# Second attention of a two-block transformer kernel: scores as two stacked products over both halves of the partitions, copies by transfers, row maxima added as a row

## The reference

```
q, k = rms_norm(q per head) * q_gain, rms_norm(k per head) * k_gain
c = cumsum(log_sigmoid(f_logit + b_f))           # one running sum per head
s = (q @ k.T) * 64**-0.5 + (c_q[:, None] - c_k[None, :])
s = where(pos_k <= pos_q, s, -inf)
p = softmax(s, axis=-1)
o = (p @ v) * sigmoid(gate);  out = o @ w_out
```

## Time and profile before

| | |
|---|---|
| runs before, median (lowest to highest) | 1735.58 us (1731.82 to 1736.38) |
| the profiled execution's own time | 1730.72 us |
| its span, first to last instruction | 1728.8 us |
| PE busy, share of the span | 1661.1 us, 96% |
| PEld / DVE / ACT / POOL busy | 79% / 53% / 36% / 6% |
| mean granted TensorE clock | 0.983 of full |
| chain of waits that ended last | PE 84%, DVE 10%, ACT 3%, issue 1%, DMA 1% |
| attention's heads in the span | about 1181 to 1316 us |

### The profile page before, as it was taken

One profiled execution on the slowest core, in us unless ns is written; L12 is line 12 of the kernel. 1 busy time (PEld: TensorE's weight loads), 2 busy tenths in 40 slices (PEclk: granted clock), 3 DMA queues, 4 the chain that ended last, 5 costly groups with the idle time before them and its releaser, 6 DMA issues.

```text
span 1728.8 us, 20336 instructions
## 1 busy us (share of the span) xinstructions
PE 1661.1 (96%) x8091; PEld 1357.3 (79%) x8091; DVE 913.3 (53%) x1256; ACT 615.5 (36%) x789; POOL 96.1 (6%) x134
## 2 busy tenths in 40 slices
PE   8899979899999899999999999999999999999997
PEld 3478858778887688888888889977877878888885
DVE  5755585577666644444344564145656544444333
ACT  2332357522223333333333443235553422222221
POOL 0100000111110000000000100003430000000000
PEclk9989989999999899999999999999999999999998
DMA  9322100555644133332333321231112333332331
GB/s 323 117 89 71 49 25 25 179 172 163 204 161 146 49 99 97 97 97 83 101 94 113 104 74 51 74 103 53 39 31 63 84 98 98 98 97 67 101 101 49
DMA packets 213924, 170.28 MB, mean 98 GB/s; under 512 B 5444, under 2 KB 202948, under 8 KB 213830
## 3 DMA queue, kind: packets, MB, share of 16 engines
q1 hardware_dynamic: 207222, 144.80, 28.2%
q0 software_dynamic: 6608, 24.19, 4.2%
HBM read 166.84 MB, written 2.13 MB: 98 GB/s over the span
## 4 chain that ended last, share of the span: by engine, by line
PE 84%; DVE 10%; ACT 3%; issue 1%; DMA 1%; DVEq 0%; SPq 0%; POOLq 0%; POOL 0%; ACTq 0%
PE PS L436 23%; PE PS L437 23%; PE PS L438 23%; PE PS L2173 2%; DVE WL L92 2%; DVE T L92 1%; PE PS L563 1%; ACT WH L88 1%; PE PS L2156 1%; PE PS L2148 1%; PE PS L2149 1%; PE PS L2150 1%; PE PS L2129 1%; PE PS L457 0%; PE PS L1188 0%
## 5 line engine op out<-in xcount | busy, mean ns | idle before, releaser
L436 PE MATMUL PS<-XH,WH 128*128 128x512 f32 (+1 forms) x1280 | 488.8, 382 | 9.3 <-DVE WL L92 8.3
L437 PE MATMUL PS<-XL,WH 128*128 128x512 f32 (+1 forms) x1280 | 485.1, 379 | 0.0
L438 PE MATMUL PS<-XH,WL 128*128 128x512 f32 (+1 forms) x1280 | 484.9, 379 | 0.0
L92 DVE TENSOR_TENSOR WL<-WS,WH 128x2048 fp32r<-128x2048 f32 (+1 forms) x129 | 272.4, 2112 | 222.8 <-ACT WH L88 220.6
L436 PEld LDWEIGHTS PS<-XH,WH 128*128 128x128 f32 x1280 | 240.6, 188 | 57.7 <-DVE WL L92 11.8
L438 PEld LDWEIGHTS PS<-XH,WL 128*128 128x128 f32 x1280 | 240.0, 188 | 45.6
L437 PEld LDWEIGHTS PS<-XL,WH 128*128 128x128 f32 x1280 | 240.5, 188 | 43.7
L88 ACT ACTIVATE WH<-WS 128x2048 fp32r<-128x2048 f32 (+1 forms) x129 | 228.6, 1772 | 74.9 <-PE PS L438 51.2
L436 PE MATMUL PS<-HH,WH 128*128 128x512 f32 x352 | 137.0, 389 | 0.2 <-DVE WL L92 0.2
L437 PE MATMUL PS<-HL,WH 128*128 128x512 f32 x352 | 136.9, 389 | 0.0
L438 PE MATMUL PS<-HH,WL 128*128 128x512 f32 x352 | 136.9, 389 | 0.0
(11 more groups left out here) (361 smaller groups left out, 2363.0 us busy)
## 6 DMA issues: line engine op xcount, KB each, us to landing
WS<-in_w_in SPq DMA_DIRECT2D x24, 1024.0 KB, 5.4
WS<-in_ffn_w_up SPq DMA_DIRECT2D x44, 512.0 KB, 5.1
WS<-in_ffn_w_in SPq DMA_DIRECT2D x44, 512.0 KB, 5.0
MSRC<-in_w_mod POOLq DMA_DIRECT2D x32, 512.0 KB, 4.8
WS<-in_fox_w_in SPq DMA_DIRECT2D x16, 1024.0 KB, 5.6
WS<-in_ffn_w_down SPq DMA_DIRECT2D x16, 704.0 KB, 4.7
WS<-in_ffn_w_out SPq DMA_DIRECT2D x16, 704.0 KB, 4.7
MODW<-in_w_mod SPq DMA_DIRECT2D x8, 1024.0 KB, 10.9
```

Source lines behind the costliest of these rows:

```text
L92: self.e.tensor_tensor(o, a, b, op).then_inc(*self.done.to(*key))
L436: e.matmul(o, lh, rh, start=first and i == 0, stop=False)
L437: e.matmul(o, lh, rl, start=False, stop=False)
L438: ins = e.matmul(o, ll, rh, start=False, stop=last and i == n - 1)
```

## The change

The scores of a tile become three products. Two tiles of both halves are stacked: `KLH[., x]` holds the low keys in the head's own half and the high keys in the other half, `QHL[., x]` the high queries in its own half and the low queries in the other, so that one product over 128 partitions gives both cross terms. `KHZ` x `QHZ` is the high product, and in the half that was zero `KHZ` has a row of ones and `QHZ` the row of bounds, so that it subtracts the bound too. `SHIFT`, `ONER`, `QS` and `KLZ` go. What lies in the wrong half is brought there by SP: six transfers for each pair (`fx_pair_load`), and four for each head (`fx_shift_load`), each of which writes 128 bounds, one from each partition, into 512 bytes of one row. VectorE copies the bounds once for them (`BTR`). The rows' products read the own half of `QHZ` and `KHZ` alone: 64 partitions. ScalarE copies the high queries in two instructions for each pair, GpSimd makes the low ones in two. SP issues decay loads, pair loads and bound loads in a new order, and chunk `OUT2 + 2` after them, as `QHZ[0]` and `QHL[0]` lie in its landing slot.

```diff
@@ fx_split_act / fx_split_dve / fx_split_pool
-        a.act(QS[m % 2][:, :], QT[:, m, :], ACT.Copy, key=("fx_q_hi", m))
+        for x in range(2):
+            a.act(QHZ[m % 2][own(x), x, :], QT[own(x), m, :], ACT.Copy, key=("fx_q_hi", m, x))
...
-        g.e.wait_ge(*acts.at("fx_q_hi", m))
-        g.tt(QO[:, m, :], QT[:, m, :], QS[m % 2][:, :].bitcast(F32), ALU.subtract, key=("fx_q_lo", m))
+        for x in range(2):
+            g.e.wait_ge(*acts.at("fx_q_hi", m, x))
+            g.tt(QO[own(x), m, :], QT[own(x), m, :], QHZ[m % 2][own(x), x, :].bitcast(F32), ALU.subtract,
+                 key=("fx_q_lo", m, x))
@@ new
+    def fx_pair_load(e, m):
+        i, done = m % 2, landing(f"fx_pair{m % 2}")
+        for x in range(2):
+            e.wait_ge(*acts.at("fx_k_hi", m, x))
+            e.dma_start(KLH[i][own(1 - x), x, :].bitcast(F32), KHZ[i][own(x), x, :].bitcast(F32)).then_inc(done, 16)
+        for x in range(2):
+            e.wait_ge(*acts.at("fx_q_hi", m, x))
+            e.dma_start(QHL[i][own(x), x, :].bitcast(F32), QHZ[i][own(x), x, :].bitcast(F32)).then_inc(done, 16)
+        for x in range(2):
+            e.wait_ge(*pool.at("fx_q_lo", m, x))
+            e.dma_start(QHL[i][own(1 - x), x, :].bitcast(F32), QO[own(x), m, :].bitcast(F32)).then_inc(done, 16)
+    def fx_shift_load(e, h):
+        m, x = divmod(h, 2)
+        r = 64 - 64 * x
+        e.wait_ge(*dve.at("fx_shift", h))
+        for i in range(4):
+            row = QHZ[m % 2][r:r + 1, x, 128 * i:128 * i + 128].bitcast(F32)
+            e.dma_start(row, BTR[:, h % 4, i:i + 1].bitcast(F32)).then_inc(landing(f"fx_shift{h % 4}"), 16)
@@ fx_rows_pe
-            q = QS[m % 2][:, 128 * i:128 * i + 128]
+            q = QHZ[m % 2][own(x), x, 128 * i:128 * i + 128]
+            k = KHZ[m % 2][own(x), x, :]
@@ fx_scores_pe
-            e.wait_ge(*pool.at("fx_q_lo", m))
+            e.wait_ge(*landed(f"fx_pair{b}", 6 * (m // 2 + 1)))
...
-            e.matmul(o, kh[:, x, k0:k1], qh[:, q0:L], start=True, stop=False)
-            e.matmul(o, kh[:, x, k0:k1], ql[:, q0:L], start=False, stop=False)
-            e.matmul(o, kl[:, x, k0:k1], qh[:, q0:L], start=False, stop=False)
+            e.matmul(o, KLH[b][:, x, k0:k1], QHL[b][:, x, q0:L], start=True, stop=False)
             e.matmul(PS[0:KEYS[t], STOFF[t]:STOFF[t] + w], IDR[:, 0:KEYS[t]], AFTER[:, c:c + w], start=False, stop=False)
             if t == 0:
-                e.wait_ge(*pool.at("fx_shift", h))
-            ins = e.matmul(o, ONER[:, 0:KEYS[t]], SHIFT[h % 2][:, q0:L], start=False, stop=True)
+                e.wait_ge(*landed(f"fx_shift{h % 4}", 4 * (h // 4 + 1)))
+            ins = e.matmul(o, KHZ[b][:, x, k0:k1], QHZ[b][:, x, q0:L], start=False, stop=True)
@@ fx_max_dve
+        if h >= 4:
+            e.wait_ge(*landed(f"fx_shift{h % 4}", 4 * (h // 4)))
+        v.cp(BTR[:, h % 4, :], BT[:, h % 2, :], key=("fx_shift", h))
@@ sync
-        for j in range(PROJ + 3, OUT2 + 3):
+        for j in range(PROJ + 3, OUT2 + 2):
...
-        for h in range(16):
+        fx_decay_load(e, 0)
+        fx_pair_load(e, 0)
+        fx_shift_load(e, 0)
+        for h in range(1, 4):
             fx_decay_load(e, h)
-        for j in range(OUT2 + 3, NCH):
+        fx_pair_load(e, 1)
+        fx_shift_load(e, 1)
+        for h in range(14):
+            if h + 4 < 16:
+                fx_decay_load(e, h + 4)
+            fx_shift_load(e, h + 2)
+            if h % 2 and (h + 3) // 2 < 8:
+                fx_pair_load(e, (h + 3) // 2)
+        for j in range(OUT2 + 2, NCH):
             load_chunk(e, j)
```

More of the change, by code:

```diff
@@ L259, in build @@
     KHZ = [zone(f"KHZ{i}", [128, 2, NT], F32R, 52.5 + 4.125 * i) for i in range(2)]
-    KLZ = [zone(f"KLZ{i}", [128, 2, NT], F32R, 60.75 + 4.125 * i) for i in range(2)]
-    IDR, ONER, AFTER = (zone(n, [128, 128], F32R, 86.5 + 0.5 * i) for i, n in enumerate(("IDR", "ONER", "AFTER")))
+    KLH = [zone(f"KLH{i}", [128, 2, NT], F32R, 60.75 + 4.125 * i) for i in range(2)]
+    IDR, AFTER = (zone(n, [128, 128], F32R, 86.5 + 0.5 * i) for i, n in enumerate(("IDR", "AFTER")))
     FG = [zone(f"FG{m}", [128, L], F32, 72.5 + 2 * m) for m in range(7)] + [T[0]]
@@ L275, in build @@
     BT = sbt("BT", [128, 2, 4], F32, TO + 4544)
+    BTR = sbt("BTR", [128, 4, 4], F32R, TO + 4576)
     FB = zone("FB", [16, NT], F32, 79.75)
@@ L278, in build @@
     FO = zone("FO", [16, NT], F32, 84.25)
-    QS = [zone("QS0", [128, L], F32R, 69), room("QS1", [128, L], F32R, 0)]
-    SHIFT = [room(f"SHIFT{i}", [128, L], F32R, 2 + 2 * i) for i in range(2)]
+    QHZ, QHL = ([sbt(f"{n}{i}", [128, 2, L], F32R, o + k * U8) for i, o in enumerate((FIX + 8 * U8, WO[1] + 8 * U8))]
+                for n, k in (("QHZ", 0), ("QHL", 4)))
     NCK = [room("NCK0", [128, NT], F32, 32), room("NCK1", [128, NT], F32, 6)]
@@ L379, in load_chunk @@
             e.wait_ge(*dve.at("na_max", 8 * (j - GATE) - 1))
+        if j == OUT2 + 2:
+            e.wait_ge(*pe.at("fx_scores", 13, 2))
         if j < RAW + 3:
@@ L403, in lo_chunk @@
         w = WH[:, place(j), 0:nk * n].bitcast(F32)
+        if j == OUT2 + 1:
+            v.e.wait_ge(*pe.at("fx_scores", 15, 2))
         v.e.wait_ge(*acts.at("wh", j))
@@ L1936, in foxp_act @@
         e.wait_ge(*landed("causal"))
-        for o, i in ((IDR, ID), (ONER, ONE), (AFTER, MASK)):
+        for o, i in ((IDR, ID), (AFTER, MASK)):
             a.act(o[:, :], i[:, :], ACT.Copy)
@@ L2090, in fx_decay_load, with own @@
             landing(f"decay{h % 4}"), 16)
+    def own(x):
+        return slice(64 * x, 64 * x + 64)
     def fx_split_act(a, m):
@@ L2098, in fx_split_act @@
         for x in range(2):
-            a.act(KHZ[m % 2][64 * x:64 * x + 64, x, :], KT[64 * x:64 * x + 64, m, :], ACT.Copy, key=("fx_k_hi", m, x))
+            a.act(KHZ[m % 2][own(x), x, :], KT[own(x), m, :], ACT.Copy, key=("fx_k_hi", m, x))
+        if m == 0:
+            a.e.wait_ge(*dve.at("wl", OUT2 - 1))
         if m == 1:
             a.e.wait_ge(*pe.at("fg", 7))
-        a.act(QS[m % 2][:, :], QT[:, m, :], ACT.Copy, key=("fx_q_hi", m))
+        for x in range(2):
+            a.act(QHZ[m % 2][own(x), x, :], QT[own(x), m, :], ACT.Copy, key=("fx_q_hi", m, x))
@@ L2104, in fx_split_dve @@
     def fx_split_dve(v, m):
         for x in range(2):
-            p0, p1 = 64 * x, 64 * x + 64
             v.e.wait_ge(*acts.at("fx_k_hi", m, x))
-            v.tt(KLZ[m % 2][p0:p1, x, :], KT[p0:p1, m, :], KHZ[m % 2][p0:p1, x, :].bitcast(F32), ALU.subtract,
+            v.tt(KLH[m % 2][own(x), x, :], KT[own(x), m, :], KHZ[m % 2][own(x), x, :].bitcast(F32), ALU.subtract,
                  key=("fx_k_lo", m))
     def fx_split_pool(g, m):
-        g.e.wait_ge(*acts.at("fx_q_hi", m))
-        g.tt(QO[:, m, :], QT[:, m, :], QS[m % 2][:, :].bitcast(F32), ALU.subtract, key=("fx_q_lo", m))
+        for x in range(2):
+            g.e.wait_ge(*acts.at("fx_q_hi", m, x))
+            g.tt(QO[own(x), m, :], QT[own(x), m, :], QHZ[m % 2][own(x), x, :].bitcast(F32), ALU.subtract,
+                 key=("fx_q_lo", m, x))
@@ L2115, in fx_rows_pe @@
+    def fx_shift_load(e, h):
[5 more added lines that the diff above has]
+            e.dma_start(row, BTR[:, h % 4, i:i + 1].bitcast(F32)).then_inc(landing(f"fx_shift{h % 4}"), 16)
     def fx_rows_pe(e, h):
         m, x = divmod(h, 2)
-        if x == 0:
-            e.wait_ge(*acts.at("fx_q_hi", m))
+        e.wait_ge(*acts.at("fx_q_hi", m, x))
@@ L2125, in fx_rows_pe @@
             if i == 3:
-                e.matmul(PS[:, o:o + 16], q, KHZ[m % 2][:, x, 0:16], start=True, stop=True)
-                e.matmul(PS[:, o + 16:o + w], q, KHZ[m % 2][:, x, 16:w], start=True, stop=False)
+                e.matmul(PS[:, o:o + 16], q, k[:, 0:16], start=True, stop=True)
+                e.matmul(PS[:, o + 16:o + w], q, k[:, 16:w], start=True, stop=False)
             else:
-                e.matmul(PS[:, o:o + w], q, KHZ[m % 2][:, x, 0:w], start=True, stop=False)
+                e.matmul(PS[:, o:o + w], q, k[:, 0:w], start=True, stop=False)
             ins = e.matmul(PS[:, o + w - 128:o + w], AFTER[:, :], IDR[:, :], start=False, stop=True)
@@ L2136, in fx_scores_pe @@
         m, x = divmod(h, 2)
-        kh, kl, qh, ql = KHZ[m % 2], KLZ[m % 2], QS[m % 2], QO[:, m, :]
+        b = m % 2
         if x == 0:
             e.wait_ge(*dve.at("fx_k_lo", m))
-            e.wait_ge(*pool.at("fx_q_lo", m))
+            e.wait_ge(*landed(f"fx_pair{b}", 6 * (m // 2 + 1)))
         if h == 0:
@@ L2246, in fx_max_dve @@
         e.wait_ge(*landed(f"decay{h % 4}", h // 4 + 1))
-        if h >= 2:
-            e.wait_ge(*pool.at("fx_shift", h - 2))
         for i in range(4):
@@ L2288, in fx_value_pool, with fx_zero_queries @@
         g.cp(VP[x][0:16, 4, 64 * x:64 * x + 64], VF[0:16, 4, 64 * h:64 * h + 64], key=("fx_v", h))
[L2290 to L2295, removed]
+    def fx_zero_queries(g, i):
+        for x in range(2):
+            g.memset(QHZ[i][own(1 - x), x, :].bitcast(F32), 0.0)
     def fox_pool(g):
```

(12 more changed lines are left out.)

## The result

Changed kernel: 1745.15 us median of six runs (1742.94 to 1751.12). Kernel before, beside it: 1733.7 us (1730.53 to 1738.9). Ratio 1.0071, 95% interval 1.0051 to 1.0091: some 12 us slower, where 2.1 were forecast. That is outside the 5.2 us either way to which the forecast gave 0.56. The profiled execution took 1745.4 us (span 1743.6), 14.8 more than that of before.

The account below looks back on a forecast made before the run. TensorE was taken as the bound in the heads, the rows-maxima-rows chain at their start. Terms -21.3 + 19.5 + 3.9 = +2.1 us gave 1737.7 us; own range 1732 to 1743, 8-in-10 range 1724 to 1748.

Parts of the forecast that it names:

- rival 2: Attention start: three TensorE pauses keep it at 1.2 GHz until scores of head 2; +10, about 1747 us, chance 0.13.
- matmul terms: TensorE in all 16 heads: scores lose products, -21.3 us, and rows gain partition-count changes, +19.5 us.
- the start: First heads of the attention: two new TensorE waits of about 1.7 us each plus 0.5 for the clock, together +3.9 us.
- Products removed: Scores of each head: two products fewer per tile, 1.33 us less per head, 16 heads, -21.3 us.
- Rows on 64 partitions: Rows of each head: eight changes of partition count at 0.20 us, 2.46 us instead of 1.24; 16 heads, +19.5 us.
- The handover: Bounds passed by VectorE copy, four issues and a landing: 6.9 us per head, hidden in the loop with 3.3 to spare.
- clock term: Rows of head 1, now longer, lie in the 3.2 us at 1.2 GHz after the 2.6 us pause: 0.5 us more.
- the second wait forecast: Scores of head 1 at the attention start: TensorE waits another 1.7 us for their bounds to land.
- Three pauses: TensorE pauses at the attention start of 2.6, 1.7 and 1.7 us within about 13 us, assumed to hold the clock down.
- Rivals 1 and 3: First: partition-count changes are free, 1718.2 us, chance 0.12; third: bounds transfers are slow, about 1796 us, chance 0.06.

Follow-up runs that it names:

- full rows: Changed kernel with the rows' products over all 128 partitions again, GpSimd zeroing the stale bounds first: 1724.99 us, ratio 0.9968 to the kernel before.
- filling the first pause: Changed kernel with full rows, decay loads ahead of head 0's bounds, and ten unused products ahead of head 1's rows: 1724.96 us, ratio 0.9956.
- filling all: Kernel with bounds ordered, plus unused products in three start pauses: ten before rows 1, ten and six before head 0's and 1's bounds-waiting products: 1720.41 us.
- bounds ordered: Changed kernel with full rows, decay loads issued ahead of head 0's bounds, and head 1's bounds ahead of pair 1's copies: 1721.33 us, ratio 0.9931.

## Why the prediction was right and where it was wrong

The time lay in the range of 1724 to 1748, but beyond the forecast's own 1732 to 1743; the case that came true is rival 2, given 0.13 (about 1747 us). In the profiled execution the matmul terms were -1.3 us (-1.8 forecast), the start +10.5 (+3.9), and dips of the clock in the later heads +5.0, a term that the sum did not have.

- *Products removed, -21.3.* Right. Between the kernel before and the one with full rows, the head at full clock goes from 7.18 to 5.82 us: 1.36, 21.8 for 16. In the changed kernel scores are 1.97 us and not 1.90, since the change into the rows stands at their end; the forecast had it in the rows.
- *Rows on 64 partitions, +19.5.* Right. A head is 1.27 us longer with eight changes than with none, 20.3 for 16; with four it is 0.64. So the cause is confirmed, not only the size: the forecast had 0.20 us for a change, the runs have 0.16. The Trainium skill, TensorEngine Tiling (Array Packing), Key Properties, says that changing the mode drains the engine, without a figure; the 0.16 us for a change fit that. How they divide into draining and weights not loaded ahead, which the forecast put at 0.09 and 0.11, no run shows. What no row of before could price, and I did not look for, is that such rows also bring dips of the clock: 5.0 us here, some 14 in the kernel before with these rows.
- *The handover.* Hidden in the running loop, as forecast: no wait for bounds after head 0. A landing took 2.0 us, not 3.2, but an issue 0.60 in place of 0.43; from the first issue, at 1184.30, to the product that waited, at 1188.18, are 3.9 us, where 1.3 + 3.2 = 4.5 were taken. The 2.0 us of the Trainium skill, DMA: Bandwidth & Descriptors, Anatomy of one DMA, which the prediction quoted, are given there for transfers that GpSimd issues; these, issued by SP, took as long.
- *The start, +3.9.* The step that failed is its clock term: "rows of head 1, now longer, lie in it: 0.5 more". The waits were 0.61 and 2.26, 2.9 against 3.4 forecast; that head 0's own bounds are waited for had been left out, and the second wait forecast, in scores 1, did not appear, with products at half speed ahead of it. But half clock lasted 23 us and cost 9.1, 7.6 more than before, where 0.5 more was forecast. I took the 3.2 us of the earlier trace rows as the length that a pause costs; it was the length behind one pause with no gap after it. The kernel before with rows on 64 partitions has changes behind that pause and no gap, and its first dip is 3.4 us too, so what was different here is the second pause.
- *Rival 2.* That pauses at the start make a long stretch at half clock is shown; its condition was wrong. "Three pauses" are not needed: one of 2.7 us and one of 0.5 do it with rows of changes, one of 2.8 and one of 0.8 with full rows. With full rows, filling the first pause only moves the stretch, and filling all removes it. That its 1747 us lie so near is luck: it took the start at about 13 us, where 10.5 were measured, and did not know the 5.0 of the dips.
- *Rivals 1 and 3* are out: changes are not free, and the bounds land in 2.0 us.

Open: what in the rows with changes makes the dips. Behind the start they fall with the number of changes (eight a head: three to nine in all four such kernels; four: a stretch behind a pause of 1.54 us only; none: none), but there is one profiled execution of each kernel, their places differ, and I have not separated the changes from the thinner stream of columns that they leave. Open too is what ends a stretch: with bounds ordered, TensorE stayed at half for 13 us of gapless work, where the same level had ended after 3.4 us in the kernel before. And a pause alone is not enough: with full rows, waits of up to 1.40 us in the running loop, at full clock, did not lower it.

## What to carry to other kernels

Price a matmul by its neighbours: on half the partitions between products over all of them each change cost about 0.16 us here, so group products of one partition count. Where a new wait stands close behind an old pause, do not take the length of the old half-clock stretch for the next: ask what it costs if the whole start of the attention runs at half speed, since that was three times the waits themselves. And look at the order on the queue that hands small transfers over: at 0.6 us an issue, putting what is waited for first, in two places, was worth about 4 us here with full rows (1724.99 to 1721.33), and nothing that could be told in the changed kernel, where only one was tried.

## What the hardware showed that was not expected

- SP's issues became slower, not only more: a decay load's issue has a median of 0.59 us, where it was 0.32 before and at most 0.43. A bounds transfer of 128 pieces of 4 bytes takes 0.60 to issue and 2.0 to land, no longer than any other copy of the loop: a pair copy of 128 KB lands in 2.4, a decay load of 264 KB in 3.5.
- The granted clock has two patterns in this stage: single dips of about 3.4 us in a busy stream with many changes of partition count, and stretches of 10 to 24 us behind pauses.
